# A 31-tap convolution by 32x32 blocks on TensorE for four of eight channel tiles, with its layer norm summed tile by tile

## The reference

```python
mod_x = (silu_c @ w_mod[i] + b_mod[i])[:, None, :]          # 6 x 1024 modulations, the same for the context
hx = rmsnorm(x, norm_g[i, 0]) * (1.0 + sc_x) + sh_x
# conv_module
u = h @ w_pw1 + b_pw1
a, gt = jnp.split(u, 2, axis=-1)
u = a * jax.nn.sigmoid(gt)
u = lax.conv_general_dilated(u, w_dw[:, None, :], window_strides=(1,), padding=[(15, 15)],
    dimension_numbers=("NWC", "WIO", "NWC"), feature_group_count=u.shape[-1]) + b_dw      # 31 taps per channel
u = jax.nn.silu(layernorm(u, ln_g, ln_b))
yx = u @ w_pw2 + b_pw2
x = x + g_x * rmsnorm(yx, norm_g[i, 1])
fx = rmsnorm(x, norm_g[i, 2]) * (1.0 + scf_x) + shf_x       # the feed-forward part follows
```

## Time and profile before

| | us |
|---|---|
| three runs | 2287.10, 2288.84, 2284.27 |
| median | 2287.1 |
| the profiled execution | 2287.43 |
| its span | 2285.7 |
| TensorE busy | 2067.9 (90%) |
| VectorE busy | 1223.0 (54%) |
| ScalarE busy | 996.6 (44%) |
| GpSimd busy | 427.1 (19%) |
| mean granted TensorE clock | 0.945 of full |

### The profile page before, as it was taken

The page is one execution under the profiler, slowest core; times in us unless marked ns, Lnnn a source line. Parts: engine busy times, 40 slices in busy tenths (PEclk is TensorE's granted clock), DMA queues, the critical chain, the costliest instruction groups (busy, mean ns, idle before and its releaser), DMA issues. The chain is left out here.

```text
span 2285.7 us, 34025 instructions
## 1 busy us (share of the span) xinstructions
PE 2067.9 (90%) x13816; PEld 1816.1 (79%) x13816; DVE 1223.0 (54%) x2436; ACT 996.6 (44%) x1814; POOL 427.1 (19%) x230
## 2 busy tenths in 40 slices
PE   5997679999997799899998879999999888999997
PEld 3853557888885666789997878989998777899997
DVE  4789335323334365364557454666455745467464
ACT  4321443232232345554444455456455445445554
POOL 0000010000001214400010111353452011153524
PEclk9998689999998899999999999999999989999999
DMA  8331433232232233365543332545654243354551
GB/s 331 101 127 57 139 129 111 93 98 96 92 102 96 83 124 122 106 201 185 183 153 125 135 114 85 169 136 175 194 175 146 77 157 103 118 171 138 191 183 58
DMA packets 84538, 307.35 MB, mean 134 GB/s; under 512 B 9376, under 2 KB 10656, under 8 KB 84000
## 3 DMA queue, kind: packets, MB, share of 16 engines
q1 hardware_dynamic: 84384, 305.19, 40.3%
HBM read 304.10 MB, written 1.05 MB: 134 GB/s over the span
## 5 line engine op out<-in xcount | busy, mean ns | idle before, releaser
L461 PE MATMUL pb<-Hh,whi 128*128 128x256 f32 (+1 forms) x2832 | 889.7, 314 | 73.0 <-DVE MOD L1752 18.7
L462 PE MATMUL pb<-Hl,whi 128*128 128x256 f32 (+1 forms) x2832 | 878.1, 310 | 0.0
L463 PE MATMUL pb<-Hh,wlo 128*128 128x256 f32 (+1 forms) x2832 | 877.5, 310 | 0.0
L1716 DVE TENSOR_TENSOR wlo<-raw,whi 128x1024 fp32r<-128x1024 f32 x325 | 407.9, 1258 | 445.4 <-ACT whi L1080 444.4
L461 PEld LDWEIGHTS pb<-Hh,whi 128*128 128x128 f32 x2832 | 555.2, 196 | 103.0 <-issue 48.0
L1080 ACT ACTIVATE whi<-raw 128x1024 fp32r<-128x1024 f32 x468 | 489.4, 1053 | 327.5 <-PE pb L463 314.3
L462 PEld LDWEIGHTS pb<-Hl,whi 128*128 128x128 f32 x2832 | 555.6, 196 | 22.6
L463 PEld LDWEIGHTS pb<-Hh,wlo 128*128 128x128 f32 x2832 | 554.8, 196 | 23.0
L2502 POOL TENSOR_TENSOR wlo<-raw,whi 128x1024 fp32r<-128x1024 f32 x143 | 343.5, 2415 | 923.5 <-ACT whi L1080 923.5
L2510 POOL TENSOR_TENSOR X<-X,tmpb 128x512 f32<-128x512 f32 (+1 forms) x12 | 16.6, 1386 | 729.1 <-DVE tmpb L1815 729.1
L1861 DVE SCALAR_TENSOR_TENSOR Y<-U,VEC,Y 128x512 f32<-128x512 f32 x180 | 120.6, 747 | 0.0
(11 more groups left out here) (279 smaller groups left out, 2619.8 us busy)
## 6 DMA issues: line engine op xcount, KB each, us to landing
raw<-wstream SPq DMA_DIRECT2D x572, 512.0 KB, 3.4
X<-xin SPq DMA_DIRECT2D x2, 1024.0 KB, 8.6
CON<-consts SPq DMA_DIRECT2D x1, 1182.0 KB, 9.4
out<-X SPq DMA_DIRECT2D x8, 128.0 KB, 1.7
VEC<-vecs SPq DMA_DIRECT2D x1, 662.0 KB, 10.6
CON<-consts SPq DMA_DIRECT2D x1, 132.0 KB, 5.7
VEC<-vecs SPq DMA_DIRECT2D x1, 88.0 KB, 2.1
```

Of the source, the lines that this page charges most:

```text
L461: e.matmul(dst, hi, xh, start=k == 0, stop=False)
L462: e.matmul(dst, hi, xl, start=False, stop=False)
L463: i = e.matmul(dst, lo, xh, start=False, stop=k == kt - 1)
L1716: e.tensor_tensor(wlo[:, i, :], raw[:, p % NRAW, :], f32(whi[:, i, :]), ALU.subtract).then_inc(sig("dve_lo", ("lo", p)), 1)
```

## The change

Tiles 4 and 5 move from VectorE to TensorE, and the form of TensorE's convolution changes. The channels of the upper half of pw1's outputs are reordered on the way in (`block_order`), so that the four rows of 32 partitions of a tile belong to four different output tiles. Each tap is then 16 products of 32x32: row r and column group ct of the array, moving operand U of tile 4 + ct, output in bank r at the partitions of ct. The blocks of taps (32x32 diagonals) are made by GpSimd, in four chunks of eight taps. As a 32nd tap a product with minus one subtracts a shift.

The norm works with this shift: the mean over tiles 0 and 1 alone, summed by TensorE after tap 8 and widened after tap 13. It is subtracted from every tile; the mean and the squares of the shifted tiles are then summed tile by tile (`norm_sums`, one moving block of 128 columns in each column group, L545's helper), so there is no centring pass. The variance is the mean square less the squared mean, on 128 columns. Scaling a tile becomes two operations of VectorE, a product and a subtraction.

Inside the loop over taps stand the ten halves of group C and the transposes of its rows. N now has the groups (0, 9) and (0, 10), F the groups (0, 11), (1, 0) and (1, 1). All columns of C and N go to one bank and are added by a single operation ahead of the scaling loop; the first add of F comes after the next modulated input. The PSUM banks are handed out anew for this stretch: one for rows, one for the columns, two for norms, four for the convolution.

```diff
-CONV_DVE = (0, 1, 2, 3, 4, 5)
-CONV_PE = (6, 7)
-CONV_ORDER = (0, 1, 2, 3, 6, 7, 4, 5)
+CONV_DVE = (0, 1, 2, 3)
...
-MOD_N = [(0, 9), (1, 1)]
-MOD_F = [(0, 10), (0, 11), (1, 0)]
+MOD_N = [(0, 9), (0, 10)]
+MOD_F = [(0, 11), (1, 0), (1, 1)]
...
-        U, DG = overlay(("U", [128, 8, 2, 286], F32), ("DG", [128, 3, CHUNK, 128], F32))
+        U, DG = overlay(("U", [128, 8, 2, 286], F32), ("DG", [128, 3, 4, CHUNK, 32], F32))
...
+        slots.place(-1, "pm", "bank", [0], [banks[0][:, :]])
+        slots.place(-1, "mods", "bank", [1], [banks[1][:, :]])
+        slots.place(-1, "norm", "bank", [2, 3], [b[:, :] for b in banks[2:4]])
+        slots.place(-1, "conv", "bank", range(4, 8), [b[:, :] for b in banks[4:8]])
...
-            for ti, k in enumerate(CONV_PE):
-                b = bank("pt", ("conv", k), ("cv", k))
-                for c, (i0, n) in enumerate(CHUNKS):
-                    w.wait_ge(*on("dg", k, c))
...
-                    dg = DG[:, (ti * len(CHUNKS) + c) % 3, :, :]
-                    for q in range(n):
-                        i = e.matmul(two(b), dg[:, q, :], U[:, k, :, i0 + q:i0 + q + T], start=i0 + q == 0, stop=i0 + q == CONVW - 1)
-                    i.then_inc(sig("pe_conv", *([("dgused", k, c)] + ([("conv", k)] if c == len(CHUNKS) - 1 else []))), 1)
-                    mod_tr(1)
-                    bite(2)
-            bite(99)
-            b = bank("pst", ("stat", "cm"), ("cent", 7))
-            for n, k in enumerate(CONV_ORDER):
-                w.wait_ge(*on("cv", k))
-                i = e.matmul(b, con("mean"), Y[:, k * 512:(k + 1) * 512], start=n == 0, stop=n == 7)
-            i.then_inc(sig("pe_stat", ("sums", "cm")), 1)
+            part[0] = -1
+            got = [bank("conv", ("conv", r), ("fin", 4 + r)) for r in range(4)]
+            mods = bank("mods", ("modtrs",), ("mods",))
+            taken = []
+            def mod_cols(n=99):
+                for l, g in ends[:n]:
+                    t = slots.at(("row", l, g))
+                    w.wait_ge(*on("row", l, g))
+                    for j in range(4):
+                        o = 8 * len(taken) + 2 * j
+                        i = e.matmul(mods[:, o:o + 2], t[:, j * 128:(j + 1) * 128], con("pick"), start=True, stop=True)
+                    i.then_inc(sig("pe_mod", ("modtr", l, g)), 1)
...
+            def norm_sums(k, first, last):
+                w.wait_ge(*on("fin", k))
+                quarters("cz", Y[:, k * 512:(k + 1) * 512], 512, first, last, ("zsum", k))
+                w.wait_ge(*on("sq", "cv", k))
+                quarters("cv", slots.at(("sq", "cv", k)), 512, first, last, ("sums", "cv") if last else ("xsum", "cv", k))
...
+            for ct in range(4):
+                w.wait_ge(*on("u", 4 + ct))
+            for i_ in range(CONVW + 1):
+                c, q = i_ // CHUNK, i_ % CHUNK
+                w.wait_ge(*on("dg", c))
+                if i_ == CONVW:
+                    w.wait_ge(*on("shift"))
+                dg = DG[:, c % 3, :, :, :]
+                for ct in range(4):
+                    for r in range(4):
+                        rows = slice(32 * r, 32 * r + 32)
+                        src = U[rows, 4 + ct, :, i_:i_ + T] if i_ < CONVW else two(slots.at("shift")[rows, :])
+                        i = e.matmul(two(got[r][32 * ct:32 * ct + 32, :]), dg[rows, ct, q, :], src, start=i_ == 0, stop=i_ == CONVW)
+                if i_ == CONVW:
+                    i.then_inc(sig("pe_conv", ("dgused", c), *[("conv", r) for r in range(4)]), 1)
+                elif q == CHUNK - 1:
+                    i.then_inc(sig("pe_conv", ("dgused", c)), 1)
+                if i_ % 3 == 2 and i_ < 30:
+                    mod_cols(1)
+                    bite(1)
+                if i_ == 8:
+                    bank("norm", ("stat", "cs"), ("root", "cs"))
+                    w.wait_ge(*on("cv", 0))
+                    quarters("cs", Y[:, 0:512], 512, True, False, ("zsum", "cs"))
+                    w.wait_ge(*on("cv", 1))
+                    quarters("cs", Y[:, 512:1024], 512, False, True, ("sums", "cs"))
+                if i_ == 13:
+                    w.wait_ge(*on("root", "cs"))
+                    widen("cs", 512, ("shift",), ring="norm")
+                if i_ == 24:
+                    bank("norm", ("stat", "cz"), ("rec", "cvm"))
+                    bank("norm", ("stat", "cv"), ("cvar",))
+                    norm_sums(0, True, False)
+                    norm_sums(1, False, False)
             feed("N")
-            b = bank("pt", ("stat", "cv"), ("root", "cv"))
-            for k in range(8):
-                w.wait_ge(*on("sq", "cv", k))
-                sums("cv", slots.at(("sq", "cv", k)), b, 512, k == 0, k == 7, ("sums", "cv") if k == 7 else ("xsum", "cv", k))
-                if k % 4 == 3:
-                    bite(1)
+            mod_cols(1)
             bite(2)
-            spread("cv", 512, [("ct", 7)])
-            bite(99)
-            mod_tr()
+            norm_sums(2, False, False)
+            norm_sums(3, False, False)
+            bite(2)
+            for k in range(4, 8):
+                norm_sums(k, False, k == 7)
+            mod_cols()
+            part[0] = 0
+            r = slots.at(("root", "cv"))
+            widen("cv", 512, ("ctm", 7), r=r[:, 0:128])
+            widen("cvm", 512, ("ct", 7), r=r[:, 128:256])
...
-            def diag(k, c):
...
-                    i = e.activation(dg[:, q, :], con("ident"), ACT.Copy, scale=vec("conv_w_dw", (i0 + q) * 8 + k))
-                i.then_inc(sig("act_diag", ("dg", k, c)), 1)
...
+            def conv_square(k):
+                t = buf(1, "sq", ("sq", "cv", k), ("sums", "cv") if k == 7 else ("xsum", "cv", k))
+                w.wait_ge(*on("fin", k))
+                e.activation(t, Y[:, k * 512:(k + 1) * 512], ACT.Square).then_inc(sig("act_sq", ("sq", "cv", k)), 1)
+            row(1, "C", 0)
+            t = buf(1, "s", ("root", "cs"), ("spread", "cs"))
+            w.wait_ge(*on("sums", "cs"))
+            e.activation(t[:, 0:128], slots.at(("stat", "cs"))[:, 0:128], ACT.Copy, scale=4.0).then_inc(
+                sig("act_root", ("root", "cs"), ("rec", "cs")), 1)
+            row(1, "C", 1)
+            t = buf(1, "s", "shift", ("conv", 3), ("fin", 3))
+            w.wait_ge(*on("spread", "cs"))
+            e.activation(t, slots.at(("spread", "cs")), ACT.Copy).then_inc(sig("act_ev", ("shift",)), 1)
+            row(1, "C", 2)
+            conv_square(0)
+            conv_square(1)
+            row(1, "C", 3)
...
             row(1, "N", 0)
-            root("cv", 4, ("spread", "cv"))
+            conv_square(2)
+            conv_square(3)
+            row(1, "N", 1)
+            for k in range(4, 8):
+                conv_square(k)
+            t = buf(1, "s", ("root", "cv"), ("spread", "cvm"))
+            w.wait_ge(*on("sums", "cv"))
+            e.activation(t[:, 256:384], slots.at(("stat", "cz"))[:, 0:128], ACT.Square).then_inc(sig("act_root", ("cm2",)), 1)
+            w.wait_ge(*on("cvar"))
+            e.activation(t[:, 0:128], t[:, 0:128], ACT.Sqrt, bias=con("eps6")).then_inc(sig("act_root", ("root", "cv")), 1)
             preload(ACT.Silu)
-            row(1, "N", 1)
...
-            left = len(taps)
-            for g, (l, q) in enumerate(MOD_C):
-                tap(len(taps) - left + (28, 40, 52, 64, 76)[g])
-                mod_add(l, q)
+            def shift(k):
+                y = Y[:, k * 512:(k + 1) * 512]
+                w.wait_ge(*on("shift"))
+                w.wait_ge(*on("cv", k))
+                e.tensor_tensor(y, y, slots.at("shift"), ALU.subtract).then_inc(sig("dve_y", ("fin", k)), 1)
+            tap(32)
+            shift(0)
+            shift(1)
             tap(len(taps))
-            for k in range(8):
-                y = Y[:, k * 512:(k + 1) * 512]
-                w.wait_ge(*on("sums", "cm"))
-                e.tensor_tensor(y, y, slots.at(("stat", "cm")), ALU.subtract).then_inc(sig("dve_x", ("cent", k)), 1)
-            rec("cv", 4)
+            shift(2)
+            shift(3)
+            for r in range(4):
+                w.wait_ge(*on("conv", r))
...
+                w.wait_ge(*on("conv", r))
+                e.tensor_scalar(Y[:, (4 + r) * 512:(5 + r) * 512], slots.at(("conv", r)), vec("conv_b_dw", 4 + r), None,
+                                ALU.add).then_inc(sig("dve_y", ("fin", 4 + r)), 1)
+            w.wait_ge(*on("cm2"))
+            e.tensor_tensor(t[:, 0:128], slots.at(("stat", "cv"))[:, 0:128], t[:, 256:384], ALU.subtract).then_inc(
...
+            e.reciprocal(t[:, 0:128], t[:, 0:128]).then_inc(sig("dve_rec", ("rec", "cv")), 1)
+            w.wait_ge(*on("rec", "cv"))
+            e.tensor_tensor(t[:, 128:256], z, t[:, 0:128], ALU.mult).then_inc(sig("dve_rec", ("rec", "cvm")), 1)
+            w.wait_ge(*on("modtr", l, q))
+            e.tensor_tensor(MOD[:, 0, 16:44, :], slots.at(("modtrs",))[:, 0:56].rearrange("p (j s) -> p j s", j=28),
...
```

(28 more changed lines are left out.)

67 lines of the change are left out of this document (32 added, 35 removed).

## The result

The changed kernel takes 2233.0 us (median of 4 runs, 2232.46 to 2234.65), the kernel before on the same chip 2286.94 (2284.27 to 2288.84): ratio 0.9762, 95% interval 0.9747 to 0.9776. I had said 2228.0 with a range of 2215 to 2262. The gain is 54 us where I had 59.

What follows compares the result with a forecast made beforehand. VectorE's taps bound the kernel to 219.4 us, the norm's chain to 245.89, a PSUM bank to 266.14. Gains of 49.9 + 6.5 + 3.1 = 59.5 us took 2287.4 to 2228 us, range 2215 to 2262.

Steps and rivals of the forecast that it cites:

- the mark for being wrong in the main point: TensorE's convolution loop, net of what stands inside it, taking more than 35 us would refute the main point.
- I take 0.86: TensorE's convolution: all sixteen tiles side by side, 0.86 us a tap, 27.5 us for 32 taps; upper bound 13.8 a tap.
- the rival of four tiles: Convolution loop: only four tiles at once, 3.4 us a tap, kernel 2310; above 2.7 a tap it shows; chance 0.08.
- The rival of the supply: Convolution loop bound by record supply: at 50 ns each 51 us instead of 27.5, kernel 2252 to 2264; chance 0.14.
- the two kinds of neighbour: Column tiles (four) and row tiles (two) each show their full factor side by side in the trace, hence 0.86 a tap.
- GpSimd beside VectorE: GpSimd builds the blocks from about 41 us while VectorE works; slowdown taken as nothing, bounds 0 and 3 us.
- The tail: Norm after the convolution, up to the first scaled tile: from 180.3 to 196 us, squares 4 to 7 behind row N1's copy.
- The third of the cold clock: Norm's tail: half TensorE clock would add 6.7 us; a third of that was taken, moving 194.0 to 196.
- pw2's stage: First scaled tile to pw2's end: 34.3 us tile loop, 25.2 products, 0.5 backlog, 60 in all against 66.5 before.
- The bank: pw2 starts with its first operand, as no modulation holds one of its first banks; that stage gains 6.5 us.
- The next norm: Norm behind pw2: VectorE's 4.09 us wait for a modulation row falls to 1.2, gain 3.1 us.
- my own range: The forecast's own range, 2216 to 2240 us, from clock, shape changes, a hidden second operation and GpSimd; chance 0.64.

## Why the prediction came out as it did

The direction, the mechanism and the likeliest case were right, and 54 of 59 us. The loop, net of what stands inside it, is 32 x 1.06 = 33.9 us, close to the 35 that I had set as the mark for being wrong in the main point. From the start of the next modulated input back, the 6.4 us that are missing there (59.5 - 53.1) lie in these terms:

- **TensorE's taps: the term that was mis-sized.** Where "I take 0.86" stands, a tap took 1.06 on average; 32 x 0.20 = 6.3 us. What stands inside the loop and the changes of shape came out 2 us cheaper, so the loop took 52.2 us, not 47.9. Sixteen tiles do run side by side, and the rival of four tiles is dead: its 3.4 us a tap and my threshold of 2.7 are far off. The rival of the supply is dead too, as 20 ns a record were seen. My argument from the two kinds of neighbour gave the factor of the columns rightly, but a row with four tiles at once can't show an extra that was seen with twelve and sixteen and not with eight. The rival of four tiles asked the right question, how far ahead TensorE looks: just far enough for one tap of sixteen, and the next tap starts 0.19 us late for it. The range for the unknown should have had such a term per tap; it had one per change of shape.
- **GpSimd beside VectorE**, taken as nothing with bounds of 0 and 3, costs 1.0 us in pw1, as shown above, and the convolution starts 1.3 us late with it. I had looked at the wrong side as well. Twelve operations of GpSimd took 9.80 us at the start. Of the four of the fourth chunk the first took 14.39 us, while VectorE's taps beside it went on every 0.66 us as if alone, and ended only behind the two subtractions; the other three took 1.0 each, and then it was VectorE's taps that were slow, four in 4.01 us:

```profile
40.78 9.80 POOL L2593 TENSOR_TENSOR DG<-CON,VEC 128x256 f32<-128x256 f32 x12 [39.28 <-DMA VEC<-vecs]
...
144.76 14.39 POOL L2593 TENSOR_TENSOR DG<-CON,VEC 128x224 f32<-128x224 f32 x1 [94.17 <-PE pb L649]
...
159.11 2.98 POOL L2593 TENSOR_TENSOR DG<-CON,VEC 128x224 f32<-128x224 f32 x3
...
158.63 4.01 DVE L1910 SCALAR_TENSOR_TENSOR Y<-U,VEC,Y 128x512 f32<-128x512 f32 x4
```

  These four are 1.3 us longer than elsewhere (0.98 us apart instead of 0.66). With the 1.1 us by which VectorE's last gated tile is late, that is why VectorE ended at 182.4, not 180.0; it was hidden behind TensorE's 3.5. It is the same in the second trace of the changed kernel (14.38 us for the first operation, 1.02 for the next three). What let the waiting operation in is not shown. Here a rule was at hand that I had not weighed: by the Trainium skill (SBUF — State Buffer, "Who interferes with whom") a VectorE operation with two SBUF inputs and a GpSimd operation that reads SBUF exclude each other for the whole instruction. The trace agrees in kind, with 14.39 us for the operation that waited; but that one waited behind some twenty operations of VectorE, not one.
- **The tail** took 14.3 us (185.83 to 200.09), 15.7 predicted. The branch was the one named: the squares of tiles 4 to 7 behind the copy of row N1. The third of the cold clock that I had added (2 us) was hardly needed, at 0.97; only the widening stood at 0.63. The sum missed a chance in the change rather than a cost: the rows were the longer branch and could move.
- **pw2's stage** took 62.4 us, 60 predicted: 35.5 to the last low part (34.3), and 1.7 instead of 0.5 for the backlog, at a clock of 0.77. The added operation stands in the serial part with its full length, as said; a tile takes 4.89 us, 4.17 + 0.72. That this serial part was an order of ScalarE and not work, I didn't see: it was worth more (11 us) than any other term that is left.
- **The bank** (6.5): taking the addition back behind the fifth tile costs 8 us.
- **The next norm**: 281.93 - 262.46 = 19.5 us instead of 22.7 (335.02 - 312.35), 3.2 against 3.1, and VectorE's wait is 1.35.

As a sum: 196 + 1.3 (start) + 4.3 (loop) - 1.4 (tail) = 200.1, up to rounding; then 2.4 (pw2) and -0.1 (norm): 6.4. With 1.9 us less behind, 2228 + 6.4 - 1.9 = 2232.5, the profiled execution's time. These 1.9 us came by luck, and the tail's 1.4 came from a margin for the clock; without both the miss would be 8 us, still inside the range. The lower end of my own range, 2216, does not follow from its terms: 2228 - 2 - 2 - 5 = 2219.

Of the two rules weighed: strict order of matmuls (the Trainium skill, TensorE: Matmul & The Clock Gate, "Part 3: Packing small matmuls — row/col tiling") would have given 6.9 us a tap; the trace shows 1.06, and 1.94 in the order made to provoke it. The 62 ns per matmul ("Wait — 56ns, not 53.3ns?" there) is 66 ns a product in the changed kernel, by chance: with half the columns the same product takes 0.63 / 16 = 39 ns, so no such floor exists here.

## What to carry to other kernels

A convolution or any other product that uses one diagonal of the array can be packed sixteenfold, at 66 ns a product of 512 f32 columns; give each tap all its tiles before the next tap comes, since products are overtaken only some sixteen deep. When a loop gets a second operation, look first whether its period is the busy time of an engine or an order of two engines: ScalarE's copy and its weights' high part moved ahead gave a fifth of what the whole change gave. An addition that frees a bank is priced by who needs the bank next. Small rows on TensorE belong where it waits anyway, each in a bank that nobody is still reading.

## What the runs showed that I had not expected

- An extra per group of side-by-side 32x32 f32 products that grows with the tiles: 0 us with 8, 0.13 with 12, 0.20 with 16, and 0.20 with half the columns too. It is a late start: the eighteenth product from the oldest unfinished one starts 0.19 us after that one is done (138.87 to 139.07).
- TensorE passes a product that waits for its own tile: two taps per tile in a row ran as eight tiles together, 1.94 us a tap, neither strict order (6.9) nor free (1.06).
- GpSimd and VectorE slow each other both ways: VectorE's low parts by 1.42 / 0.87 beside GpSimd's building, and one GpSimd operation took 14.39 us beside an unbroken row of VectorE's taps, where the next three took 1.0 each.
